# The queue's order in the first state-space steps, and one weight tile ahead of small products in the third step

## The reference

```python
xn = rmsnorm(h, g_pre)
uz = xn @ w_in
u, z = jnp.split(uz, 2, axis=-1)
y = s5_ssm(u, ...)   # h_t = Abar h_{t-1} + Bbar u_t, 128 groups of 16 channels; y = Re(C h) + D u
y = jax.nn.gelu(y)
y = y * jax.nn.sigmoid(y @ w_glu + b_glu)
y = y * jax.nn.silu(z)
return h + rmsnorm(y @ w_out, g_post)
```

## Time and profile before

| | |
|---|---|
| median of 3 runs | 3070.48 us (3069.7 to 3071.14) |
| profiled execution | 3066.98 us, its span 3065.2 us |
| TensorE busy | 2982.9 us, 97% |
| VectorE, ScalarE, GpSimd busy | 44%, 39%, 53% |
| granted TensorE clock, mean | 0.989 |
| DMA, mean | 114 GB/s |

### The profile page before, as it was taken

One profiled execution on the slowest core, in us unless ns is written; L12 is line 12 of the kernel. 1 busy time (PEld: TensorE's weight loads), 2 busy tenths in 40 slices (PEclk: granted clock), 3 DMA queues, 4 the chain that ended last, 5 costly groups with the idle time before them and its releaser, 6 DMA issues.

```text
span 3065.2 us, 53484 instructions
## 1 busy us (share of the span) xinstructions
PE 2982.9 (97%) x21192; PEld 2376.1 (78%) x21192; DVE 1360.0 (44%) x2166; ACT 1187.9 (39%) x1640; POOL 1639.3 (53%) x1355
## 2 busy tenths in 40 slices
PE   7899999999899999999999999999999999998997
PEld 5778888888788888888888878777777777775686
DVE  8788861120443132222322046456456455466612
ACT  5455653243533232323333254343343343344521
POOL 4455544454777777777773464444444444344342
PEclk9999999999999999999999999999999999998998
DMA  4566673242222222222222242222222222225522
GB/s 171 171 198 203 204 205 149 96 151 96 70 90 93 95 89 86 89 100 88 89 86 91 98 149 97 82 104 77 85 106 73 90 98 80 91 77 162 167 96 96
DMA packets 128935, 347.97 MB, mean 114 GB/s; under 512 B 61936, under 2 KB 65008, under 8 KB 98304
## 3 DMA queue, kind: packets, MB, share of 16 engines
q1 hardware_dynamic: 128784, 345.73, 33.7%
HBM read 306.07 MB, written 35.55 MB: 111 GB/s over the span
## 4 chain that ended last, share of the span: by engine, by line
PE 49%; issue 25%; POOL 20%; DVE 4%; ACT 2%; DMA 1%; SPq 0%; POOLq 0%; DVEq 0%; ACTq 0%
POOL wlo L173 16%; PE bank L196 14%; PE bank L198 14%; PE bank L197 14%; POOL g L2001 2%; PE bank L1408 1%; PE bank L1390 1%; PE bank L2106 1%; POOL wk L644 1%; PE bank L1399 1%; PE bank L2180 0%; DMA wraw<-in_wall_dram 0%; PE bank L2146 0%; POOL wk L638 0%; ACT whi L168 0%
## 5 line engine op out<-in xcount | busy, mean ns | idle before, releaser
L173 POOL TENSOR_TENSOR wlo<-wraw,whi 128x512 fp32r<-128x512 f32 (+1 forms) x896 | 1181.5, 1349 | 1171.8 <-ACT whi L168 1171.7
L196 PE MATMUL bank<-rhi,whi 128*128 128x512 f32 x3632 | 1455.9, 401 | 42.8 <-POOL wlo L173 28.0
L197 PE MATMUL bank<-rlo,whi 128*128 128x512 f32 x3632 | 1419.6, 391 | 0.0
L198 PE MATMUL bank<-rhi,wlo 128*128 128x512 f32 x3632 | 1419.1, 391 | 0.0
L196 PEld LDWEIGHTS bank<-rhi,whi 128*128 128x128 f32 x3632 | 683.8, 188 | 217.2 <-issue 40.2
L198 PEld LDWEIGHTS bank<-rhi,wlo 128*128 128x128 f32 x3632 | 684.0, 188 | 145.8
L197 PEld LDWEIGHTS bank<-rlo,whi 128*128 128x128 f32 x3632 | 684.9, 189 | 136.9 <-issue 4.3
L168 ACT ACTIVATE whi<-wraw 128x2048 fp32r<-128x2048 f32 (+2 forms) x227 | 428.2, 1887 | 450.7 <-PE bank L198 272.2
L1182 POOL TENSOR_TENSOR wraw<-wraw,vec 128x512 f32<-128x512 f32 x248 | 252.1, 1047 | 0.0
L961 DVE TENSOR_TENSOR ssum<-ssum,wk 128x512 f32<-128x512 f32 x28 | 20.6, 737 | 278.1 <-ACT wk L951 278.1
L2001 POOL TENSOR_TENSOR g<-g,wk 128x256 f32<-128x256 f32 x80 | 58.8, 757 | 108.9 <-PE bank L1774 57.5
(11 more groups left out here) (385 smaller groups left out, 3056.1 us busy)
## 6 DMA issues: line engine op xcount, KB each, us to landing
wraw<-in_wall_dram SPq DMA_DIRECT2D x223, 1024.0 KB, 4.9
g<-in_bmat_dram SPq DMA_DIRECT2D x16, 512.0 KB, 3.9
g<-scr_e SPq DMA_DIRECT2D x128, 64.0 KB, 3.0
scr_a<-ssum SPq DMA_DIRECT2D x24, 256.0 KB, 2.3
g<-in_xp_dram SPq DMA_DIRECT2D x4, 1024.0 KB, 11.8
g<-in_cmat_dram SPq DMA_DIRECT2D x16, 256.0 KB, 7.0
scr_u<-wk SPq DMA_DIRECT2D x16, 256.0 KB, 2.6
scr_y<-wk SPq DMA_DIRECT2D x16, 256.0 KB, 3.2
```

The lines of the kernel that those rows point to most:

```text
L173: ins = pool.tensor_tensor(wlo[:, slot, c], wraw[:, slot, c], whi[:, slot, c].bitcast(F32), ALU.subtract)
L196: pe.matmul(out[:, :], whk, rhi[:, k, :], start=(k == first), stop=False)
L197: pe.matmul(out[:, :], whk, rlo[:, k, :], start=False, stop=False)
L198: ins = pe.matmul(out[:, :], wlk, rhi[:, k, :], start=False, stop=(k == last))
```

## The change

Two edits in the written-out first steps; the steps in the loop and the last ones stay as they are.

1. In step 0, SP issues weight tile 7, the `cq` of block 1 and the `ug` of block 0 ahead of its wait for the factors, instead of behind the loads of `et` and the store of a z tile.
2. In step 2, TensorE projects u tile 7 ahead of the kernels' products of block 1, instead of behind them.

```diff
--- before.py
+++ after.py
@@ -336,6 +336,15 @@
             sp.wait_ge(w_lo, low)
             w_load(sp, n, slot)
 
+        def c_load(sp, j):
+            sp.wait_ge(q_rdy, j + 1)
+            sp.dma_start(m["cq"], a["cmat"][j + 1]).then_inc(cq_in, 16)
+
+        def ug_load(sp, j, u):
+            wait(sp, yq, j - 1)
+            sp.wait_ge(u_wr, 16 * j + 16)
+            sp.dma_start(ug[u], scr_u[j].rearrange("s (c g) k -> (s c) (g k)", g=GT)).then_inc(ug_in[u], 16)
+
         def sp_step(sp, j, u, h, lo, hi):
 
             if u == 0:
@@ -354,6 +363,9 @@
                 sp.dma_start(m["bt"], a["bmat"][:, bass.ts(j, 1024)] if not isinstance(j, int) else
                              a["bmat"][:, j * 1024:(j + 1) * 1024]).then_inc(be_in, 16)
                 if lo == 0:
+                    w_load_after(sp, u_tile(0, 0) + 3, 0, u_tile(0, 0) + 3)
+                    c_load(sp, 0)
+                    ug_load(sp, 0, 0)
                     sp.wait_ge(e_rdy, E_STEPS)
                     sp.dma_start(scr_e.rearrange("s g n -> g s n"),
                                  wk[:, 4224:5248].rearrange("p (s n) -> p s n", s=L)).then_inc(e_wr, 16)
@@ -377,18 +389,15 @@
                 tv = m["tt"].rearrange("p (g n) -> p g n", g=GT)
                 for s in range(L):
                     sp.dma_start(tv[s * SC:(s + 1) * SC, :, s * SC:P], kv[:, :, 0:P - s * SC]).then_inc(t_in, 16)
-            if hi <= 15:
-                wait(sp, yq, j - 1)
-                sp.wait_ge(u_wr, 16 * j + 16)
-                sp.dma_start(ug[u], scr_u[j].rearrange("s (c g) k -> (s c) (g k)", g=GT)).then_inc(ug_in[u], 16)
+            if hi <= 15 and lo > 0:
+                ug_load(sp, j, u)
             if lo >= 2 and hi <= 17:
                 sp.wait_ge(yg_rdy, j - 1)
                 sp.dma_start(scr_y[j - 2].rearrange("s (c g) k -> (s c) (g k)", g=GT), m["yg"]).then_inc(yg_wr, 16)
-            if hi <= 15:
+            if hi <= 15 and lo > 0:
                 w_load_after(sp, u_tile(u, h) + 3, 0, u_tile(u, h) + 3 - u)
-            if hi <= 14:
-                sp.wait_ge(q_rdy, j + 1)
-                sp.dma_start(m["cq"], a["cmat"][j + 1]).then_inc(cq_in, 16)
+            if hi <= 14 and lo > 0:
+                c_load(sp, j)
             if lo == 15:
                 sp.wait_ge(yg_wr, 64)
                 for t in range(4):
@@ -532,6 +541,8 @@
             return ins
 
         def pe_step(pe, j, u, h, lo, hi):
+            if lo == 2:
+                project(pe, u_tile(u, h), 0)
             if lo >= 1 and hi <= 16:
                 t, v = j - 1, 1 - u
                 pe.wait_ge(q_rdy, t + 1)
@@ -541,7 +552,7 @@
                     ins = pe.matmul(ps_k[q:q + SC, g // 4 * P:(g // 4 + 1) * P], m["bb"][:, g * SC:(g + 1) * SC],
                                     q1[v][:, g * 144:g * 144 + P], start=True, stop=True)
                 ins.then_inc(k_mm, 1)
-            if hi <= 16:
+            if hi <= 16 and lo != 2:
                 project(pe, u_tile(u, h), 0)
             has_y, has_x = lo >= 2 and hi <= 17, lo >= 1 and hi <= 16
             if has_y:
```

## The result

The changed kernel takes 3076.16 us (median of 18 runs, 3073.48 to 3081.56), the kernel before beside it 3070.03 us (18 runs, 3063.41 to 3073.89). The ratio is 1.0023, with a 95% interval of 1.0016 to 1.0030: **slower by some 7 us** (the medians differ by 6.1). The forecast was 3069.8 us and no change, its range ended at 3072.7.

What follows compares the result with a forecast made beforehand. TensorE, busy 97% of the span, was taken as the bound, so only its idle or half-clock time could be won. The round's 0.8 us less 0.1 gave 0.7, 3070.48 - 0.7 = 3069.8 us; range 3066.3 to 3072.7.

Steps and rivals of the forecast that it cites:

- D: SP's queue, step 0: delay of the factors' store behind the transfers moved ahead of it; 1.9 us, bounds 0 and 3.2.
- The wait for L426: TensorE, start of step 2: its 5.8 us wait for `dve_out` on VectorE would be gone.
- the stall moves: TensorE, step 2: idles some 5 us ahead of block 1's x products in place of ahead of tile 7.
- rival (c): Block 0's x products: a wait near 4 us brings half clock, round 2.2 us late, 3072.7 us; chance 0.09.
- T: VectorE: time at which `p` of block 1 is ready, 125.3 + D = 127.2 us; block 1's x products wait for it.
- The round: VectorE's evacuation of tile 7 and the chain it starts: begins 0.8 us sooner, priced as a 0.7 us gain.
- rival (d): Block 1's x products: half clock after the new wait, TensorE's lag not absorbed; 3070.5 to 3071 us, chance 0.27.
- SP itself loses nothing: SP, step 0: its three moved issues are over long before 93 us, so they cost SP no time.
- the 106: Landing of `et`: after 106 us the prediction is wrong and (c) holds; 103 to 105 was expected.
- (a): SP's queue: the factors' store is not delayed, D near 0, the round gains 2.7 us; 3067.8 us, chance 0.12.
- (b): Ahead of block 1's x products: the new wait is short, TensorE gets back 7.5 us; 3063.0 us, chance 0.07.
- the 9.4 us: TensorE around step 2's start: all that can be won, 0.8 + 5.8 + 0.7 of idling and 2.1 of half clock.

Runs made afterwards that it cites:

- second execution of the changed kernel: The changed kernel profiled once more with no edit, without the early lateness of its first profile; 3074.67 us.
- first execution of the changed kernel: The first profile of the changed kernel, late already before the change's place; 3081.56 us, 5.4 above the median.
- ballast: Kernel before plus a 1.5 MB memory-to-memory copy of weights, issued ahead of the wait for the factors; ratio 1.0007 (0.9998 to 1.0017).
- split after `p`: Changed kernel with one more wait: GpSimd starts tile 7's split only when `p` of block 0 is made; ratio 1.0032 (1.0020 to 1.0044).

## Why the prediction was wrong

**What held.** The queue: D was forecast at 1.9 us, with bounds of 0 and 3.2; counted from the end of the factors it is 2.3 in the second execution of the changed kernel and 2.8 with edit 1 alone. The tile's rounding at 100 (99.35) and its readiness at 107.6 (107.49). The wait for L426 gone. Above all that the stall moves: the copy of block 1's kernels waits for the late products (126.76, after 16 us of idling), `p` of block 1 stands behind it, and TensorE waits ahead of the x products, 4.60 us against some 5 forecast.

**The step that failed** is the one that reads "The x products of block 0 start at 106.30 + D: TensorE's 0.80 us of waiting become 2.7." It took `p` of block 0 to last 4.07 us, as in a trace in which GpSimd stood idle beside it. The same prediction put the split of tile 7 at 102 to 107.6, beside `p`, and did not price that. It lasts 7.35 us, the x products start at 111.16 and TensorE waits 6.41 us. That the neighbour does this was tried from both sides: taken away, `p` is 4.07 again; put into the kernel before, it is 6.61.

The trace of the kernel before had shown such a price, some 15 us ahead of `p`. There VectorE's last products for the factors, also 128 x 256 with both inputs in SBUF, begin beside GpSimd's split of tile 6 (to 88.83 us) and the instruction behind it (to 90.00):

```profile
87.75 1.36 DVE L691 TENSOR_TENSOR wk<-wk 128x256 f32<-128x256 f32 x1 [0.16 <-DVE wk L489]
89.14 1.15 DVE L692 TENSOR_TENSOR wk<-wk 128x256 f32<-128x256 f32 x1
90.33 0.43 DVE L693 TENSOR_TENSOR wk<-wk 128x256 f32<-128x256 f32 x1
```

**The half clock follows**, in the place that rival (c) named and for another reason (there the delay of the factors should have caused it). Stretches of the second execution of the changed kernel, with TensorE's clock before the DMA share:

```profile
core 0: us, PE busy (x) PEld busy (x) DVE busy (x) ACT busy (x) POOL busy (x), PEclk, DMA share, GB/s
...
110.50:117.00 6.50, 5.74 (x73) 4.72 (x74) 6.21 (x8) 0.20 (x1) 4.81 (x4) 0.52 0.64 168
118.00:122.00 4.00, 4.00 (x19) 3.30 (x19) 3.77 (x6) 0.00 (x0) 0.00 (x0) 1.00 0.41 84
```

The x products of block 0 take 2.36 us in place of 1.48, and tile 7 takes 126.06 - 113.45 = 12.6, as long as before, where the forecast had 10.9. So the sum is, from the forecast T = 127.2 for the x products of block 1: + 3.3 (`p`: 7.35 - 4.07), + 0.9 and + 1.7 (half clock), + 0.4 (D: 2.3 in place of 1.9), - 0.7 (this execution was ahead), 132.8. Measured: 132.73.

**The round** on VectorE, which I took as the price, starts at 132.59 in place of 128.03: 4.6 us late (5.3 from block 0's kernels' products) where 0.8 were to be won. The new wait ahead of block 1's x products was followed by half clock too (a granted clock of 0.50 from 133 to 136.3), as rival (d) said: the z tile comes 136.35 - 132.73 = 3.6 us behind them in place of 1.98. With the 4.5 us by which those come late, from block 0's kernels' products, that makes 6.2 us at the z tile, beside 6.1 by the medians and 7 by the ratio, whose interval is 5 to 9. The forecast had most of a lag of TensorE absorbed further on; the runs do not show that.

**"SP itself loses nothing"** failed in the first execution of the changed kernel, where the wait for tile 6's split held the factors' store for 2.5 us (94.28 against 91.8). It held in the second, so it depends on how late GpSimd is. In the first execution `et` landed at 107.93, past the 106 that the prediction had named as its sign for (c); in the second at 103.67, short of it.

**The rivals.** (a) and (b) fell: D was not near 0, and TensorE got back nothing of the 9.4 us. (c) and (d) each named half of what happened, and both were priced without the long `p`. That edit 2 alone would cost 8 us no rival had; the prediction's own chain gives it once tile 7 is late, and half clock is counted twice. Two of the prediction's sums are off, without effect: the chances of its cases add up to 1.00 before the 0.04 for the unseen, and the 1.3 us that it estimates for D leave out the 0.2 us that its 1.9 takes off.

## What to carry to other kernels

Before a step is moved into an idle stretch of one engine, look at who works beside it: an instruction's duration in the trace holds for its neighbours in that trace, and VectorE's products of 128 x 256 with both inputs in SBUF got up to 3.5 times as long (1.49 us in place of 0.43) beside GpSimd. On VectorE such a loss shows as busy time, not as a wait, so a list of its waits does not name it; compare the mean of the same instruction in two stretches. And when products are put behind a long tile so that they do not stall it, follow the chain that starts at them to its end: here the next stall was waiting behind the copy.

## What the runs showed of the hardware that was not expected

VectorE's products of 128 x 256 with both inputs in SBUF take 0.43 us alone and mostly 1.27 to 1.5 us beside GpSimd's subtractions of 128 x 512 (some 1.3 us each), and the one of 128 x 1152 takes 1.35 or 2.43 us, by which of the two engines began first. Instructions with one input from PSUM did not change: 0.69 us. The Trainium skill, "SBUF — State Buffer", section "Who interferes with whom", states that such a two-input instruction contends with a GpSimd instruction that reads SBUF, as its second input comes through a read interface that the two share, and that one with at most one SBUF input does not contend; its section "Summary: rules for kernel authors" adds that the second to issue is blocked until the first has finished. The traces agree: the 1.27 to 1.5 us are about one piece of GpSimd's split, 1.35 or 2.43 us goes by who began first, and 0.69 us stays. The prediction had looked for a rule against the change on the DMA's side, where the price was small.

The other: a wait of TensorE of 3.6 us (ballast) and one of 3.60 (split after `p`) were followed by half clock (a granted clock of 0.50 from 109.3 to 111.3 and from 108.9 to 110.9; the x products took 2.36 and 2.35 us); those of 0.80 to 1.53 us ahead of the same products, in the kernels without a delay, were not (1.00, 1.48 us).
